# A two-layer streaming encoder whose second layer leaves out 12 of its 592 frames from the queries on

## The reference, cut to what matters

```
proj = rmsnorm(x) @ w_in          # q, k, v; B, C, h of a short conv; a GLU pair; three gates
y_attn = attention(q, k, v) @ w_attn_out          # chunks of 64 frames, window of 128, per-head sinks
y_sc   = (sc_b * conv3(sc_c * sc_h)) @ w_sc_out   # causal depthwise conv, width 3
y_cf   = silu(layernorm(conv31(a * sigmoid(g)))) @ w_cf_out
x += (g_attn * y_attn + g_sc * y_sc + g_cf * y_cf) @ w_o
h  = rmsnorm(x) @ w_up                            # 2 * 2816 channels
x += (silu(conv3(h)[:2816]) * conv3(h)[2816:]) @ w_down
```

## Time and profile before

| | |
|---|---|
| median of 3 runs | 2571.84 us (2571.27 to 2581.23) |
| profiled execution: its time, its span | 2571.93 us, 2570.8 us |
| mean granted clock of TensorE | 0.978 of full speed |
| PE busy | 2512.2 us, 98% of the span |
| DVE busy | 1644.4 us, 64% |
| ACT busy | 859.2 us, 33% |
| weights by SP | 350 transfers of 512 KB, 3.3 us to landing (median) |

### The profile page before, as it was taken

The page is one execution under the profiler, slowest core; times in us unless marked ns, Lnnn a source line. Parts: engine busy times, 40 slices in busy tenths (PEclk is TensorE's granted clock), DMA queues, the critical chain, the costliest instruction groups (busy, mean ns, idle before and its releaser), DMA issues.

```text
span 2570.8 us, 47457 instructions
## 1 busy us (share of the span) xinstructions
PE 2512.2 (98%) x17842; PEld 2478.5 (96%) x17842; DVE 1644.4 (64%) x2466; ACT 859.2 (33%) x1616; POOL 114.6 (4%) x207
## 2 busy tenths in 40 slices
PE   7998999999999999999999999999999999999997
PEld 6998899999999999999999888999999999999996
DVE  8787667776534663645787875777764356546366
ACT  4124332223523442423432243222235234324243
POOL 0032100000000000000000321000000000000000
PEclk9997899999999999999999988999999999999998
DMA  4220022222233222222232200222222322222223
GB/s 181 82 87 15 8 74 82 77 78 83 81 99 96 83 74 82 82 82 82 92 117 77 82 1 24 76 81 82 82 75 88 104 91 75 82 82 80 76 82 105
DMA packets 57621, 204.35 MB, mean 79 GB/s; under 512 B 8335, under 2 KB 8399, under 8 KB 57263
## 3 DMA queue, kind: packets, MB, share of 16 engines
q1 hardware_dynamic: 52560, 190.03, 22.6%
q0 software_dynamic: 4960, 12.94, 1.7%
HBM read 193.14 MB, written 8.50 MB: 78 GB/s over the span
## 4 chain that ended last, share of the span: by engine, by line
PE 94%; DVE 4%; ACT 1%; issue 1%; DMA 0%; POOL 0%; DVEq 0%; ACTq 0%; SPq 0%; POOLq 0%
PE ps L473 81%; PE ps L502 5%; PE ps L588 4%; PE ps L552 2%; PE ps L567 1%; PE ps L569 1%; DVE w_lo L1014 1%; DVE cf_acc L1062 0%; PE ps L600 0%; ACT w_hi L761 0%; PE ps L513 0%; DMA scratch<-scratch 0%; DVE xn_lo L1113 0%; DVE scratch L1028 0%; DVE x_q_merged L1509 0%
## 5 line engine op out<-in xcount | busy, mean ns | idle before, releaser
L473 PE MATMUL ps<-xn_hi,w_hi 128*128 128x296 f32 x3584 | 784.4, 300 | 2.9 <-DVE w_lo L1014 2.9
L1014 DVE TENSOR_TENSOR w_lo<-raw,w_hi 128x1024 fp32r<-128x1024 f32 x350 | 429.1, 1226 | 553.7 <-ACT w_hi L761 553.0
L473 PE MATMUL ps<-xn_hi,w_lo 128*128 128x296 f32 x3584 | 780.9, 299 | 0.0
L473 PE MATMUL ps<-xn_lo,w_hi 128*128 128x296 f32 x3584 | 779.3, 299 | 0.0
L761 ACT ACTIVATE w_hi<-raw 128x1024 fp32r<-128x1024 f32 x348 | 368.9, 1060 | 1203.5 <-PE ps L473 1135.2
L473 PEld LDWEIGHTS ps<-xn_hi,w_hi 128*128 128x128 f32 x3584 | 583.3, 189 | 4.0 <-DVE w_lo L1014 3.1
L473 PEld LDWEIGHTS ps<-xn_lo,w_hi 128*128 128x128 f32 x3584 | 584.9, 189 | 0.0
L473 PEld LDWEIGHTS ps<-xn_hi,w_lo 128*128 128x128 f32 x3584 | 581.0, 188 | 0.0
L1062 DVE SCALAR_TENSOR_TENSOR cf_acc<-glu,vec,cf_acc 128x622 f32<-128x622 f32 x368 | 295.6, 861 | 0.0
L473 PE MATMUL ps<-branch_hi,w_hi 128*128 128x296 f32 x1296 | 284.7, 301 | 0.3
L473 PE MATMUL ps<-branch_hi,w_lo 128*128 128x296 f32 x1296 | 282.0, 299 | 0.0
(11 more groups left out here) (161 smaller groups left out, 2314.5 us busy)
## 6 DMA issues: line engine op xcount, KB each, us to landing
raw<-in_weights SPq DMA_DIRECT2D x350, 512.0 KB, 3.3
spill<-x_q_merged POOLq DMA_DIRECT2D x2, 2368.0 KB, 9.6
x_q_merged<-spill POOLq DMA_DIRECT2D x16, 296.0 KB, 3.2
x_q_merged<-in_xt SPq DMA_DIRECT2D x4, 592.0 KB, 8.2
out_y<-x_q_merged SPq DMA_DIRECT2D x8, 296.0 KB, 2.3
scratch<-scratch POOLq DMA_DIRECT2D x72, 18.5 KB, 2.8
con<-in_consts SPq DMA_DIRECT2D x1, 592.0 KB, 11.5
vec<-in_vecs SPq DMA_DIRECT2D x1, 576.0 KB, 5.0
```

The lines of the kernel that those rows point to most:

```text
L473: last = nc.tensor.matmul(out[:, h, :], a[:, s, wk], b[:, k, t0 + h * n:t0 + (h + 1) * n], start=(k == 0 and j == 0), stop=(k == nk - 1 an ...
L1014: return V.tensor_tensor(wl[:, s, :], raw[:, s, :], f(wh[:, s, :]), ALU.subtract).then_inc(lo_done, 1)
```

## The change

One number moves. For the second layer `first` becomes 16 - 2 * (3 - 1) = 12, and for what follows the second layer too (the final norm), since `first` takes the second entry there:

```diff
-KEEP0 = (0, 0)
+KEEP0 = (0, N_META - 2 * (FFN_K - 1))
```

## The result

The changed kernel takes 2566.25 us (median of 20 runs, 2560.42 to 2577.54), the kernel before, timed in turn with it, 2580.31 us (median of 20, 2571.27 to 2588.2). The ratio is 0.995 with a 95% interval of 0.994 to 0.996: 10.3 to 15.5 us less. One disturbed run of 6114 us is left out. The forecast was 2553.5 us with a range of 2551.0 to 2560.5, so the direction was right and the size was not.

What follows compares the result with a forecast made beforehand. The prediction held the second layer, from its queries on apart from attention, bound by PE's panel matmuls; -18.5 + 0.2 + 0.1 - 0.1 - 0.2 = -18.5 us from 2571.93 gave 2553.5 us, range 2551 to 2560.5.

Steps and rivals of the forecast that it cites:

- What bounds the kernel: Second layer from its queries on, apart from attention: time is panel matmuls times their pace, 7392 matmuls affected.
- one cycle a column over a constant, 6 / 2.4 = 2.5 ns ... I take the last: Second-layer panel matmuls: six columns less save 2.5 ns each, 18.5 us over 7392; chance of the forecast case 0.72.
- The rival of blocks: Second-layer panels: moving data read in blocks of 4 columns, saving 1.67 ns a matmul, 12.3 us, giving 2559.6; chance 0.09.
- No change: Second-layer panels: pace not set by columns, only ends of chains saved, -0.3, giving 2571.6 us; chance 0.12.
- The odd start is slow: Second halves beginning at 302 read at a worse rate; 8.5 ns lost on each gives 2585 us; chance 0.04.
- A part is absorbed by waits: Second-layer loops: waits take up part of the saving, giving 2556 to 2571 us; chance 0.03.
- the product waits: PE's two waits for ConvFFN products: matmul cover shrinks by 90 ns, adding 0.1 us.
- the ends of `two_panels`: Last 18 matmuls covering the next panel's preparation: cover shrinks 45 ns at five places, adding 0.2 us.
- The end as a whole: Chain through DVE, ACT and PE after the last matmul, with reciprocal and eight scalings: 0.2 us shorter.
- The profiled execution took 2571.93 us, as good as the median of 2571.84: Whole kernel: the base from which the forecast savings were subtracted, 2571.93 us.
- 24 matmuls in 3.22 us: ConvFFN sign that the forecast is right: 290-column matmuls at 134.2 ns each, granted clock 1.00.
- The first layer's end at the same times as before: Sign that the forecast is right: first layer's end and second layer's queries not moved in time.

Runs made afterwards that it cites:

- uneven: Changed kernel's 580 frames cut 292 + 288 instead of 290 + 290, results laid end to end: 2553.19 us, ratio 0.9916 to the kernel before.
- swap: Changed kernel's 580 frames cut 288 + 292 instead of 290 + 290, border at 300, results laid end to end: 2547.63 us, one run.
- shift2: Kernel before with the moving tiles 8 bytes further in SBUF (padding also moves the weights 128 bytes): 2604.54 us, ratio 1.0091.
- wshift2: Kernel before with the weights w_hi and w_lo laid 8 bytes further in SBUF; padding moves tiles behind them: 2600.46 us, ratio 1.0083.
- wshift4: Kernel before with the weights laid 16 bytes further in SBUF; padding moves tiles behind them: 2580.28 us, one run.
- k8: Changed kernel with 584 frames instead of 580, halves of 292 columns beginning at 8 and 300: 2569.3 us, one run.
- starts: Changed kernel with both 290-column halves beginning on a multiple of 4 columns and ending off one, timing only: 2559.82 us, one run.
- ends: Changed kernel with both 290-column halves ending on a multiple of 4 columns and beginning off one, timing only: 2569.52 us, one run.
- before2: Kernel before, unchanged, run again for a second profile: 2580.39 us.
- wshift16: Kernel before with the weights laid 64 bytes further in SBUF; padding moves tiles behind them: 2568.89 us, single time.
- k4: Changed kernel with 588 frames instead of 580, halves of 294 columns beginning at 4 and 298: 2588.04 us, one run.

## Why the prediction was wrong

**What bounds the kernel: right.** From the queries on, apart from attention, time is the number of panel matmuls times their pace. 7392 x 1.67 = 12.3 us; the last panels gave 11.3 of it, and the nine panels' stretch of queries and values went from 59.0 to 58.4 us: 11.9 together. PE found no new wait.

**The step that failed: "one cycle a column over a constant, 6 / 2.4 = 2.5 ns ... I take the last".** It measured 1.67 ns, four cycles for six columns, so 18.5 us became 12.3. The nearest rows had been plain float32 matmuls of 144 and 192 columns, all of whole lines, which could not show what a line border costs. Nor did the constant stay, as the step assumes: it was 32 cycles before, is 34 after, and 28 in *uneven*. The second half of the changed kernel begins at 302, and the first ends there, inside a line: with the border at 304, *uneven* saves 4.17 ns a matmul with the same columns. So the loss against the forecast is at that border, and more than the loss: at clean borders even one cycle a column would have been too little.

**The rival of blocks** (1.67 ns, 12.3 us) named the right size and the cause, in part: what is paid goes with lines of 4 columns. On the moving side *uneven* and *swap* against after show the border as the cause, at 5 to 6 cycles a matmul together with what the new place brings; *shift2* gives about 4. On the weights' side *wshift2* against *wshift4* gives 4 in panels that read `xn`, and none is seen in the `w_o` panels. As a rule with a constant of 32 cycles it fails in *k8*, *k16*, *uneven* and *swap*, which are 1.5 to 4 cycles faster. Here the Trainium skill bears on it (SBUF — State Buffer, Specifications): lines of 16 bytes, with a penalty at each cross to a new line. The runs agree for the moving columns, where borders 8 bytes off a multiple of 16 stand at 33.3 cycles and more over the columns. The 28 to 32 cycles that are left do not follow from that.

**The other rivals.** "No change" fell with the pace of 135.0. "The odd start is slow" needed 8.5 ns a second half to be slower than before; odd borders cost *after* 2.5 ns a matmul against *uneven*, and starts and ends share it. "A part is absorbed by waits" is small: *uneven* should save 29.0 us over its last panels by its rows (6960 x 4.17) and saved 27.6. Of the 1.4 us that are missing the lower clock has none, since the granted clock of the stage is 1.00 in both. About 0.4 are in the 384 matmuls of the `w_o` panels (133.6 ns in place of 132.5), and about 0.5 in the pauses between panels: starts over 0.3 us apart sum to 8.3 us before and 8.9 in *uneven*.

**The small terms.** The reciprocal became 0.07 us shorter and the eight scalings 0.09 (forecast 0.08 and 0.1); the product waits are equal to a tenth; the five panels after the ends of `two_panels` started 1.2 us late in all before, counted beyond one pace, and 1.3 after (forecast 0.2 more). All of it is below what the whole time can show. The end as a whole, forecast 0.2 us shorter, was 0.9 longer in the profile, with the channel sum at the lower clock.

**The second step that failed: "The profiled execution took 2571.93 us, as good as the median of 2571.84".** Of the three runs and the profile three had fallen at the fast end (2571.27 to 2571.93 us) and one at 2581.23; the median of 20 is 2580.31. So the base was unlucky as well as taken from too few runs. *before2* shows a longer execution with panels as fast: its start and its two attentions are 8.2 us longer. With the measured pace and that median the sum is 2580.3 - 12.3 = 2568.0 us; 2566.25 was measured. Of the 12.8 us between forecast and result 6.2 come from the size of the saving and 8.4 from the base, less 1.8 that stay open, within the spread of the runs. Taken singly, the measured saving on the old base gives 2559.6 us and the forecast saving on the right base 2561.8: the base was the larger error.

**What would show it.** "24 matmuls in 3.22 us" was wrong and "3.24 us (blocks)" came. "The first layer's end at the same times as before" was wrong too: the first `two_panels` row of the second layer starts at 1284.19 before and at 1293.82 after. Most of that is the first attention (7.9 us), whose length goes with the clock that it is granted, and that differs between executions of one program.

**Open.** Why whole-line cuts differ by up to four cycles (28 in *uneven*, 32 before), why 64 bytes of weights (*wshift16*) win two cycles, and why the start of the kernel (granted clock 1.00 before, 0.98 in *before2*, 0.99 after, over the first 190 us) and attention get different clocks in different executions. Moving tiles one by one was not tried. One lead is in the traces: starts inside a panel are not evenly spaced. In *wshift2* rows of two matmuls lie 0.27 to 0.30 us apart, in an order that comes back every 24 matmuls, that is every four slices, so its price of four cycles is a mean over a few long distances and many short ones.

## What to carry to other kernels

Cut the moving columns so that each matmul begins and ends on a multiple of 16 bytes, even if the halves become unequal, and keep the weights on such a multiple: here 292 + 288 columns run 2.5 ns a matmul faster than 290 + 290, and weights 8 bytes off cost 1.6 ns in most panels. When a forecast prices a width, see where each piece begins and ends, since the nearest row may have cleaner borders than the change. Judge a change below 1% by the pace in a long loop and by cutting the span into stages; one whole time against another here mixes in up to 15.6 us of attention (265.5 us for both in the first profile, 281.1 in *k4*) whose code is the same.

## What the hardware showed that was not expected

- A border inside a 16-byte line goes with about four cycles more of a panel matmul at the 2.4 GHz level, for the moving columns (331.7 cycles with tiles 8 bytes off, 328 before) and for the weights (332 with 8 bytes off, 328 with 16), though not in the `w_o` panels (weights 8 bytes off: 327). In the rows at 1.2 GHz the 290 columns of the changed kernel cost 291 cycles, borders inside lines and all.
- 580 columns on whole lines cost 28 cycles a matmul over the columns, 592 columns 32, and the same 592 with the weights 64 bytes further 30: place in SBUF beyond 16 bytes moves the pace of the same matmuls by 0.6%.
- Results laid end to end on both sides of the border of two PSUM banks leave the pace at 136.7 ns.
- The same attention code took 132.4 to 140.9 us, with granted clocks of 0.83 to 0.77 in the windows around it.
